# Output and state-space stage in one block; the second layer's embedding product joined to the last head pair

## What is computed

```python
x = x + merged @ w_out[layer]
return rmsnorm(x, g_final)
...
for i in range(DEPTH_2):
    if i < N_A:
        h = h + mamba2_mixer(h, ...)
    else:
        k, v = shared_kv(h, kv_norm, w_kv, k_g)
        h = h + stick_breaking_mixer(h, k, v, ...)
    h = per_layer_embedding(h, p[i], ple_norm[i], ple_gate[i], ple_proj[i])

def per_layer_embedding(h, p_i, norm_g, w_gate, w_proj):
    return h + (p_i @ w_proj) * jax.nn.sigmoid(rmsnorm_2(h, norm_g) @ w_gate)
```

## Time and profile before

| | us |
|---|---|
| median of 3 runs | 3284.34 (3283.6 to 3288.83) |
| the profiled execution, its own time | 3283.73 |
| its span | 3282.3 |
| PE busy | 3098.2 (94%) |
| DVE, ACT, POOL busy | 1825.8, 1387.3, 682.7 |
| stage_out and group 0 to its z tiles | 1285.0 to 1487.2 |
| the last head pair of stage_stick | 2984 to 3050 |
| the last stage (layer 1 embedding) | 3157 to 3282 |

### The profile page before, as it was taken

How to read it: one execution, slowest core, us unless ns; L and a number is a source line. 1 busy time by engine, 2 the same in 40 slices (tenths; PEclk the granted TensorE clock), 3 DMA queues, 4 the chain that set the end, 5 groups by cost and what they waited for, 6 DMA issues and landing times. The chain is left out here.

```text
span 3282.3 us, 40235 instructions
## 1 busy us (share of the span) xinstructions
PE 3098.2 (94%) x15516; PEld 2584.3 (79%) x15516; DVE 1825.8 (56%) x2488; ACT 1387.3 (42%) x2094; POOL 682.7 (21%) x455
## 2 busy tenths in 40 slices
PE   6999998999999999998999999998899999997798
PEld 5788887888888877776787878776688888886677
DVE  4244222666676533255757566575457777776343
ACT  4333221555555423334244252434246666666231
POOL 3110001222223100302001020100234444443110
PEclk8999999999999999999999999999899999998899
DMA  2111212112111234112121121211211111111321
GB/s 93 41 51 49 71 64 71 59 55 68 58 52 65 84 110 145 44 34 71 39 71 52 46 81 41 77 46 58 79 45 40 39 39 39 39 41 43 122 77 52
DMA packets 55861, 201.14 MB, mean 61 GB/s; under 512 B 6544, under 2 KB 9616, under 8 KB 55440
## 3 DMA queue, kind: packets, MB, share of 16 engines
q1 hardware_dynamic: 46288, 166.36, 15.0%
q0 software_dynamic: 9408, 32.51, 3.2%
HBM read 167.26 MB, written 23.20 MB: 58 GB/s over the span
## 5 line engine op out<-in xcount | busy, mean ns | idle before, releaser
L114 ACT ACTIVATE whi<-wraw 128x1024 fp32r<-128x1024 f32 x208 | 218.4, 1050 | 445.9 <-PE a_D L127 59.4
L119 DVE TENSOR_TENSOR wlo<-wraw,whi 128x1024 fp32r<-128x1024 f32 x173 | 232.5, 1344 | 154.3 <-ACT whi L114 153.2
L125 PE MATMUL ssm_D<-x1hi,whi 128*128 128x512 f32 x640 | 259.7, 406 | 14.6 <-issue 9.8
L125 PE MATMUL b_D<-x1hi,whi 128*128 128x512 f32 x640 | 255.2, 399 | 8.5 <-DVEq L1006 6.6
L127 PE MATMUL ssm_D<-x1hi,wlo 128*128 128x512 f32 x640 | 251.9, 394 | 0.0
L126 PE MATMUL ssm_D<-x1lo,whi 128*128 128x512 f32 x640 | 251.9, 394 | 0.0
L126 PE MATMUL b_D<-x1lo,whi 128*128 128x512 f32 x640 | 250.8, 392 | 0.0
L127 PE MATMUL b_D<-x1hi,wlo 128*128 128x512 f32 x640 | 250.8, 392 | 0.0
L2365 DVE TENSOR_TENSOR_SCAN stick_keep<-stick_keep 128x896 f32<-128x896 f32 (+7 forms) x128 | 215.1, 1681 | 43.8 <-ACT stick_keep L2273 42.5
L2504 POOL TENSOR_TENSOR stick_rows<-stick_rows,stick_keep 128x896 f32<-128x896 f32 (+7 forms) x128 | 162.8, 1274 | 271.8 <-DVE stick_keep L2365 271.5
L125 PE MATMUL stick_D<-x1hi,whi 128*128 128x512 f32 x512 | 210.4, 411 | 6.8 <-DVE x1lo L152 6.8
(11 more groups left out here) (443 smaller groups left out, 7942.1 us busy)
## 6 DMA issues: line engine op xcount, KB each, us to landing
wraw<-w_dram SPq DMA_DIRECT2D x208, 512.0 KB, 3.5
sq<-acum_rows SPq DMA_DIRECT2D x32, 512.0 KB, 3.8
att_bias<-alibi_dram SPq DMA_DIRECT2D x16, 512.0 KB, 3.6
stack<-stack POOLq DMA_DIRECT2D x32, 256.0 KB, 3.7
x_sb<-xT_dram SPq DMA_DIRECT2D x8, 512.0 KB, 9.6
branch_a<-sq POOLq DMA_DIRECT2D x8, 512.0 KB, 3.5
y_b<-att_y POOLq DMA_DIRECT2D x8, 512.0 KB, 3.0
f<-y_b SPq DMA_DIRECT2D x2, 2048.0 KB, 8.8
```

The source lines that it names most:

```text
L114: act.activation(self.whi[:, s, :, :], self.wraw[:, s, :, :], ACT.Copy).then_inc(self.w_hi, 1)
L119: dve.tensor_tensor(self.wlo[:, s, :, :], self.wraw[:, s, :, :], self.whi[:, s, :, :].bitcast(F32), ALU.subtract).then_inc(self.w_lo, 1)
L125: pe.matmul(out, self.whi[:, s, w0, :], xhi[:, k, cols], start=start, stop=False)
```

## The change

Three things are done.

1. `stage_out` and `stage_ssm` share one block; the `clear_semaphores` between them moves ahead of `stage_out`. The last output tile is written out as eight steps over k that each give `x_free`; when PE has read tile k of `x1hi` and `x1lo` for the last time, ACT and DVE write the state-space stage's parts for k into it. Only the last k waits for the last sum. The two last additions of squares go from POOL to DVE.
2. In group 0 `spread_factor` comes four units earlier, and DVE's extra steps move from behind the taps to behind the first or second scaling (`opening`), one `final_norm` at a time.
3. The embedding product of layer 1 goes into the last head pair: `p` and `w_ple` are loaded into `f_sb`, split into `x1hi` by ACT (slots 2, 3) and DVE (slots 3, 4), and sixteen half tiles (`embed_half`, 6 matmuls each) stand behind `score` in slots 4 to 18. ACT copies each from PSUM, SP stores it to DRAM; the last stage loads it back (8 loads of 512 KB) and has no `ple_pP` product.

The core of the diff, with indentation reduced:

```diff
+x_free = sem("x_free")
+def add_tile(dve, n):
+    dve.wait_ge(mm, n + 1)
+    dve.wait_ge(x_land[n], 16)
+    dve.tensor_tensor(f_sb[:, n, :], D[:, n % 2, :], f_sb[:, n, :], ALU.add).then_inc(added, 1)
+    K.split_lo(dve, n // 2 + (n0 // 2 + 1), n % 2)
...
-with nc.Block() as block:
...
+if n < KT - 1:
...
+for k in range(KT):
+    for half in range(2):
+        last = K.products(pe, D[:, 1, half * H:half * H + H], 1, k, k, xhi, xlo, half, k == 0, k == KT - 1)
+    last.then_inc(x_free if k < KT - 1 else mm, 1)
...
-    for n in range(KT):
+for n in range(KT - 1):
...
-if n == KT - 1:
-    break
...
-    for n in range(KT):
-        dve.wait_ge(mm, n + 1)
-        dve.wait_ge(x_land[n], 16)
-        dve.tensor_tensor(f_sb[:, n, :], D[:, n % 2, :], f_sb[:, n, :], ALU.add).then_inc(added, 1)
-        K.split_lo(dve, n // 2 + (n0 // 2 + 1), n % 2)
+for n in range(KT - 1):
+    add_tile(dve, n)
...
+return mm, added, acc_done, x_free, add_tile
...
+pe.wait_ge(out_added, KT)
...
-    units(g, 0, KT, 2 * KT)
+units(g, 0, KT, KT + 4)
...
+units(g, 0, KT + 4, 2 * KT)
...
+if k < KT - 1:
+    act.wait_ge(x_free, k + 1)
+else:
+    act.wait_ge(out_mm, KT)
+    K.split_hi(act, n0 // 2, 1)
+    act.wait_ge(out_added, KT)
...
+act.wait_ge(out_acc, 2 * (KT - 2) - 1 + i)
...
+if k == KT - 1:
+    add_tile(dve, k)
...
+dve.wait_ge(out_acc, 2 * (KT - 2))
+for i, acc in enumerate((K.acc, K.R)):
+    dve.wait_ge(sq_base, i + 1)
+    dve.tensor_tensor(acc[:, :], acc[:, :], K.sq[:, i, :], ALU.add).then_inc(acc_base, 1)
...
-    def final_norm(k0, k1):
+def final_norm(k):
...
-for k in range(k0, k1):
...
+def opening(c, half):
+    if half == 0 and c == 1:
+        step_sizes()
+    if half == 0 and c == 3:
+        decay_sums()
+    if half == 0 and c == 4:
+        decay_ends()
+    if c >= 2:
+        final_norm(2 * (c - 2) + half)
...
+if g == 0:
+    opening(c, half)
...
-if g == 0:
-    if c == 0:
-        step_sizes()
-    elif c == 2:
-        decay_sums()
-    elif c == 3:
-        decay_ends()
-    if c >= 2:
-        final_norm(2 * c - 4, 2 * c - 2)
...
-for i, acc in enumerate((K.acc, K.R)):
-    pool.wait_ge(sq_base, i + 1)
-    pool.tensor_tensor(acc[:, :], acc[:, :], K.sq[:, i, :], ALU.add).then_inc(acc_base, 1)
...
+EMBED_HALVES = {4: (0,), 5: (1,), 6: (2,), 7: (3,), 8: (4,), 9: (5,), 10: (6,), 11: (7,), 12: (8,), 13: (9,),
+            14: (10,), 15: (11,), 16: (12,), 17: (13,), 18: (14, 15)}
...
+e_land, e_high, e_low, e_mm, e_copy = sem("e_land"), sem("e_high"), sem("e_low"), sem("e_mm"), sem("e_copy")
+e_left = [sem("e_left0"), sem("e_left1")]
+e_raw = [f_sb[:, 2 * i:2 * i + 2, :] for i in range(2)]
+e_hi, e_lo = ([x[:, 2 * i:2 * i + 2, :] for i in range(2)] for x in (xhi[:, 0:4, :], xhi[:, 4:8, :]))
+e_w = [t[1].rearrange("p a (b m) -> p (a b) m", m=P).rearrange("p (j k) m -> p j k m", k=2) for t in (e_hi, e_lo)]
...
+sp.dma_start(e_raw[0], io["pT"][1].rearrange("(k p) t -> p k t", p=P)).then_inc(e_land, 16)
+sp.dma_start(e_raw[1].rearrange("p a (b m) -> p (a b) m", m=P).rearrange("p (j k) m -> p j k m", k=2),
+             io["w_ple"][1].rearrange("j p k m -> p j k m")).then_inc(e_land, 16)
+sp.wait_ge(e_low, 2)
...
+for j in range(KT):
+    sp.wait_ge(e_copy, 2 * j + 2)
+    sp.dma_start(embed[j, :, :], K.sq[:, j % 2, :]).then_inc(e_left[j % 2], 16)
...
+for q in e_left:
+    sp.wait_ge(q, 16 * (KT // 2))
...
+def embed_half(n):
+    j, half = n // 2, n % 2
+    if n == 0:
+        pe.wait_ge(e_low, 2)
+        pe.wait_ge(evac, 8 * PAIRS + 2)
+    elif n >= 2:
+        pe.wait_ge(e_copy, n - 1)
+    cols = slice(half * H, half * H + H)
+    for k in range(2):
+        pe.matmul(D[:, cols], e_w[0][:, j, k, :], e_hi[0][:, k, cols], start=k == 0, stop=False)
+        pe.matmul(D[:, cols], e_w[0][:, j, k, :], e_lo[0][:, k, cols], start=False, stop=False)
+        last = pe.matmul(D[:, cols], e_w[1][:, j, k, :], e_hi[0][:, k, cols],
+                         start=False, stop=k == 1)
+    last.then_inc(e_mm, 1)
...
+if not more:
+    for n in EMBED_HALVES.get(slot, ()):
+        embed_half(n)
...
+def embed_copy(n):
+    j, half = n // 2, n % 2
+    cols = slice(half * H, half * H + H)
+    act.wait_ge(e_mm, n + 1)
+    if n >= 4:
+        act.wait_ge(e_left[j % 2], 16 * (j // 2))
+    act.activation(K.sq[:, j % 2, cols], D[:, cols], ACT.Copy).then_inc(e_copy, 1)
...
+if not more:
+    if slot in (2, 3):
+        act.wait_ge(e_land, 32)
+        act.wait_ge(dn, 8 * PAIRS)
+        act.activation(e_hi[slot - 2], e_raw[slot - 2], ACT.Copy).then_inc(e_high, 1)
+    for n in EMBED_HALVES.get(slot - 1, ()):
+        embed_copy(n)
...
+if not more:
+    for n in EMBED_HALVES[18]:
+        embed_copy(n)
...
+if not more and slot in (3, 4):
+    dve.wait_ge(e_high, slot - 2)
+    dve.tensor_tensor(e_lo[slot - 3], e_raw[slot - 3], e_hi[slot - 3].bitcast(F32),
+                      ALU.subtract).then_inc(e_low, 1)
...
+else:
+    for j in range(KT):
+        sp.dma_start(unused[:, j, :], embed[j, :, :]).then_inc(e_land[j], 16)
...
+if embed is not None:
+    if j == 0:
+        K.norm_spread(pe, spread, rtok_done, 1, spread_done)
+    continue
...
-dve.wait_ge(pm, n + 1)
...
-dve.tensor_tensor(gate[:, s, :], pP[:, s, :], gate[:, s, :], ALU.mult).then_inc(gated, 1)
+if embed is None:
+    dve.wait_ge(pm, n + 1)
+    product = pP[:, s, :]
+else:
+    dve.wait_ge(e_land[n], 16)
+    product = unused[:, n, :]
+dve.tensor_tensor(gate[:, s, :], product, gate[:, s, :], ALU.mult).then_inc(gated, 1)
...
-stage_out(K, f_sb, xhi, xlo, x_dram, decay)
...
-stage_ssm(K, xhi, xlo, f_sb, decay, *heads, acum_dram)
+with nc.Block() as block:
+    before = stage_out(K, block, f_sb, xhi, xlo, x_dram, decay)
+    stage_ssm(K, block, before, xhi, xlo, f_sb, decay, *heads, acum_dram)
```

More of the change, by code:

```diff
@@ new lines, in _ @@
+        @block.scalar
+        def _(act):
+            for k in range(KT):
+                K.tile_hi(act, xhi, f_sb, k, None, x_hi)
+            act.wait_ge(landed, 48)
+            act.activation(decay.hi[:, :, :], raw[:, :, :], ACT.Copy).then_inc(w_done, 1)
+            act.activation(decay.expA[:, :], decay.head[:, 1, :], ACT.Exp)
+            for n in range(KT - 1):
+                act.wait_ge(mm, n + 1)
+                K.split_hi(act, n // 2 + (n0 // 2 + 1), n % 2)
+                act.wait_ge(added, n + 1)
+                for i in range(2):
+                    if n >= 2:
+                        act.wait_ge(acc_done, 2 * n + i - 3)
+                    act.activation(K.sq[:, i, :] if n else accs[i][:, :], f_sb[:, n, :], ACT.Square,
+                                   scale=K.gain("g_final", n) if i else 1.0).then_inc(sq_done, 1)
@@ new lines, in _ @@
+        @block.vector
+        def _(dve):
+            for k in range(KT):
+                K.tile_lo(dve, xlo, xhi, f_sb, k, None, x_hi, x_lo)
+            dve.wait_ge(w_done, 1)
+            dve.tensor_tensor(decay.lo[:, :, :], raw[:, :, :], decay.hi[:, :, :].bitcast(F32), ALU.subtract)
+            dve.tensor_tensor(decay.gain[:, :], K.vec[:, VEC["g_final"]:VEC["g_final"] + KT],
+                              K.vec[:, VEC["m_norm"]:VEC["m_norm"] + KT], ALU.mult)
+            for n in range(KT - 1):
+                add_tile(dve, n)
@@ L1311, in stage_ssm @@
+        return mm, added, acc_done, x_free, add_tile
+def stage_ssm(K, block, before, xhi, xlo, f_sb, decay, dt, dte, acum, e_acum, e_end, acum_dram):
     nc, io, n0 = K.nc, K.io, FIRST["ssm"]
+    out_mm, out_added, out_acc, x_free, add_tile = before
     with ExitStack() as ctx:
@@ new lines, in _, with group, load, row @@
+        @block.sync
+        def _(sp):
+            def group(g):
+                def load(m):
+                    n = GROUP_TILES * g + (n0 + m)
+                    sp.wait_ge(K.w_lo, n + 1)
+                    K.load_weight(sp, n + 2, m % 2)
+                def row(c):
+                    if c == 0:
+                        sp.wait_ge(cv_d, 18 * g + 18)
+                    if c >= 2:
+                        sp.wait_ge(s2, 8 * g + (c - 1))
+                    sp.dma_start(E[c % 2], acum_dram[c, bass.ds(8 * g, GH), :]
+                                 .partition_broadcast(P)).then_inc(row_land[c % 2], 16)
+                for m in range(7):
+                    load(m)
+                    if g == 0 and m == 4:
+                        sp.wait_ge(copied, 3)
+                        sp.dma_start(acum_dram.rearrange("c h t -> h c t"),
+                                     rows[:, :].rearrange("h (c t) -> h c t", c=NC)).then_inc(stored, 16)
+                        sp.wait_ge(stored, 16)
+                for c in range(NC):
+                    row(c)
+                    if c % 2 == 1:
+                        load(7 + c // 2)
+                for m in range(11, 14):
+                    load(m)
+            for g in range(GROUPS):
+                group(g)
```

1075 lines of the change are left out of this document (516 added, 559 removed).

## The result

The changed kernel takes 3249.71 us (median of 4 runs, 3247.37 to 3252.66), the kernel before 3284.63 in the same comparison: a ratio of 0.9892, with a 95% interval from 0.9875 to 0.9909, 35 us less. The forecast was 3249.7. That the total was met is luck in good part: two of the terms were wrong by 2 to 3 us, in opposite directions, and parts of the program that the change doesn't touch moved by about as much. The profiled execution of the changed kernel (3247.37 us) even lies 1.7 us under the forecast of 3249.1 for it; the median lies 2.3 above that execution, where the forecast had added 0.6.

The account below looks back on a forecast made before the run. PE, busy 94% of the span, was taken as the bound. Terms +1.2 - 8.3 - 14.8 - 2.8 - 20.5 + 10.6 = -34.6 us gave 3249.1 for the profiled execution, 3249.7 as median; range 3244 to 3260.

Parts of the forecast that it names:

- The block end: Output stage to decay tile: clearing ahead of the output stage costs +1.2 us, decay tile without a pause gains -8.3.
- Group 0: Decay tile to z tiles: 79.4 us instead of 94.2, pause before the z tiles 2.0 instead of 9.81: -14.8 us.
- Rival B: Group 0: DVE is the bound, its waits and a fallen clock cost more; 3255.5 us, chance 0.18.
- The clock at the z tiles: Matmuls behind the pause before the z tiles: the clock stays up after 2.0 us, -2.8 us.
- 0 if it falls: Z tiles: the gain is 0 instead of -2.8 us if the clock falls behind the pause.
- The last stage: Last stage: seven tiles lose 12 matmuls each, the `w_lo` wait goes, 0.4 at the eighth tile: -20.5 us.
- The last pair: Last head pair: 7.0 us pause before the first half, restart at lower clock, 15 halves nearly free: +10.6 us.
- I take 1.0 for each: Last pair: contention with POOL lengthens each of DVE's two low parts by 1.0 us, making the pause 7.0.
- My bound of 0 from below: Last pair: lower end of the 0 to 1.68 us allowed for POOL contention on each DVE low part.
- rival A: Last pair hides more: pause 5.0 us, the clock holds, cost 6.4; 3245.5 us, chance 0.13.
- C: Last pair: halves do not overlap, held back by ACT's copies; slower than before, 3299 us, chance 0.03.
- D: Block end: x1 parts come late, the pause moves behind the decay tile, all 8.3 may go; 3258 us, chance 0.05.

Follow-up runs that it names:

- e1: Kernel before with only part 1 of the change (joined block; old group 0 order, no embedding move): 3280.2 us, ratio 0.9983.
- e3: Kernel before with only part 3 of the change, the embedding product in the last head pair: 3270.9 us, ratio 0.9960.
- c0: The changed kernel itself measured once more, as the measure for kernels beside it: 3249.06 us, ratio 0.9889.
- e4: Changed kernel with DVE's two low parts one slot earlier, in slots 2 and 3: 3244.45 us, ratio 0.9877.
- e10: Changed kernel; DVE's low parts in slots 2-3, norm wait at ssm_pY's overwrite, both ACT high parts in slot 2, last half behind PE's last product: 3236.60 us.
- e2: Changed kernel without the embedding move (joined block and new group 0 order only): 3262.7 us, ratio 0.9927.

## Why the prediction was right, and where it wasn't

**The block end.** Right in mechanism and nearly in size: -7.37 for -8.3, by e1 alone -7.5. The output stage's pause is longer by the clearing as forecast (1.07 for 1.2). Two things were missed. Behind that pause PE stayed at the low clock for 10.5 matmuls instead of 6.5, 0.8 us. That is not the pause's doing: e3 has the old pause of 6.42 and over 12 slow matmuls; the profile of before was a lucky one there. And the decay tile took 11.3 us, not 10.9. Both the forecast and the -7.37 lean on that one profile: against e3, which has the same code there as the kernel before, the difference is -9.35.

**Group 0.** The walk of DVE against PE held: a pause of 2.13 us for 2.0, no wait for a scaling, each norm where it was put. The gain is 1.3 us larger since the small sums ran at the full clock (1.93 us for the second row of sums that had taken 2.93), a term that I had left as it was; e1 shows that it comes with the joined block. What the new order itself gives, 14.6 us, is the forecast's 14.8. Rival B, DVE as the bound, falls.

**The clock at the z tiles.** The step "A pause of 2.0 is nearest to that one: -2.8 (0 if it falls)" failed. The clock fell in all seven profiles with this pause (17.85 to 17.94 us for the stretch in each), and the gain was 1.04 us. It was not 0 either, as the "0 if it falls" would have it: the mean granted clock of the stretch was 0.90 where it had been 0.85. The reading of the earlier trace rows was right, the clock had stayed behind the 2.57 us pause; to take one profile for a rule was the fault. Behind the same pause it fell in e1 and e3, so of three profiles the one that I had was the exception. The runs do not show what decides it. My unit was a little off too: at the lower clock two matmuls of 512 columns start 0.427 us apart (e1, first output tile), 1.9 times 0.227 and not twice.

**The last stage.** -21.07 for -20.5, 10.88 us a tile as forecast. The tail is as worked out: the last product waits for the sigmoid alone.

```profile
3236.55 1.06 ACT L2775 ACTIVATE sq<-sq 128x1024 f32<-128x1024 f32 x1 [9.82 <-DVE sq L2820]
...
3237.64 1.23 DVE L2830 TENSOR_TENSOR sq<-f,sq 128x1024 f32<-128x1024 f32 x1 [1.12 <-ACT sq L2775]
```

**The last pair.** The mechanism was right, a wait for the second low part and then 15 halves for nothing (0.3 us against my 0.4). The term was mis-sized: 7.63 for 10.6. The failed step is "I take 1.0 for each": DVE came first both times, so the contention fell on POOL and cost DVE nothing. My bound of 0 from below was the truth, and with it the 5.0 us of rival A (4.70 measured). The restart cost 1.0 us, not 1.9: the first half took 2.38 us instead of 1.36 (c0: 2.60). Rival A's other half, that the clock holds, did not come true; it does in e4 and in e10.

**Rivals C and D** fall: the only wait of a half in the pair is the 4.70 us of the first, so ACT's copies never held one back, and the decay tile has no wait for the parts of x1.

**What cancelled.** The pair was 3.0 us cheaper than forecast and group 0 1.3 better, the clock at the z tiles 1.8 and the block end 0.9 worse. The rest is no work of the change: 1.5 us less ahead of the output stage, 2.2 more in the rest of the state-space stage, and 0.4 to 0.6 in three others. The stretch from the z tiles to the first embedding stage, the same code but for the pause ahead of it, took 739.8 us (before), 741.0 (changed), 744.8 (c0, the same kernel as changed), 744.8 (e1) and 746.6 (e2), with short drops of the clock at other places in each. Even the start to the first output tile differs by 4.4 us between the kernel before and e3 (1285.04 and 1280.60), with the same code. So a single profile can't tell 5 us in the span. A stretch of 80 us repeats to 0.1 us where the clock behaves alike (78.04 to 78.08 in the seven profiles with the new order and its pause), and is off by 1 to 2 where it doesn't (94.14 and 95.72 for group 0 of the kernel before, 80.56 and 81.62 for the pair): read the granted clock beside the length.

## What to carry to other kernels

Cut both traces at the same points of the program and compare stretch by stretch, with the granted clock of each: it shows errors that cancel in a total, and effects of 2 to 4 us that are hard to tell by the medians of a handful of runs. Where a term rests on the clock behind a short pause, look at that pause in more than one profile. Work moved into TensorE's own waits can be nearly free even where it is longer than they are (here 20.4 us of halves for some 15.6 of waits), since it also keeps TensorE's clock up; the same work behind the last product costs what its store sticks out at the stage's end. Make inputs of such work while their engine idles, one slot before they are asked for, and put a wait where its resource is overwritten, not at the head of the phase.
